# Attention of a two-layer encoder: modulation blocks every third step instead of every second, and the first branch weight block rounded four steps later

## The chip, the cores and the metric

The kernel runs on one core of a Trainium2 chip. The metric is the device time of one execution in microseconds. Three runs of the kernel before took 1734.79 us in the median (1731.39 to 1736.03).

## The reference, cut to what matters

Two groups of 256 tokens each go through two layers with shared weights. Each layer computes six modulation vectors from a small condition vector, then an attention with two branches, then a mixture of experts:

```python
mod = jax.nn.silu(c) @ w_ada + b_ada                     # 1024 x 6144 weights
shift1, scale1, gate1, shift2, scale2, gate2 = split(mod, 6)
h = rms_norm(x, norm_attn) * (1 + scale1) + shift1
qa, ka, va, qb, kb, vb, gates = split(h @ w_in)
ya = gqa_attention(rope(norm(qa)), rope(norm(ka)), va) @ w_branch_a      # branch A: 8 heads of 64
p  = softmax(q1 k1 + bias) - lam * softmax(q2 k2 + bias)                 # branch B: 4 heads, two maps each
yb = (rms_norm(p @ vb, subln_b) * (1 - lam_init)) @ w_branch_b
merged = (sigmoid(g_a) * ya + sigmoid(g_b) * yb) @ w_out
x = x + gate1 * merged
h2 = rms_norm(x, norm_ffn) * (1 + scale2) + shift2
x = x + gate2 * grouped_moe(h2)
```

`shift1` and `scale1` are needed ahead of the attention. `gate1`, `shift2`, `scale2` and `gate2`, two thirds of the product with `w_ada`, are needed only behind it.

## The kernel before, in words

Every engine runs one program in order; engines wait for each other on semaphores. SP issues the weight loads, each of 2 MB, into six slots (`ring`); the order of the blocks is written out in `SLOT`, and a block that reuses a slot is loaded when TensorE has counted the last one there as used.

The product with `w_ada` is cut into 12 blocks of 512 columns. The first four are done ahead of the attention, blocks 4 to 11 in it. A block has three parts. *Rows*: eight accumulating products of 32 output rows each, run as matmuls into one PSUM bank (L750), then ScalarE copies the bank to `tmp` (L1187, function `ada_copy`). *Columns*, one step later: four transposes of `tmp` into another bank (L758). *Sum*, another step later: VectorE adds the four partial rows up into `mod` (L1579, function `ada_sum`), waits for its own result, and gives the bank free (L1581).

The attention is a list of 24 units in 28 steps. Units 0 to 15 belong to branch A (a head pair's half and a token group; one map), units 16 to 23 to branch B (two maps). A step i holds, on TensorE and in this order: the scores of unit i (L887), the turn (transposes) of unit i-2's probabilities (L896), the values product of unit i-3 (L909), for branch B the sum of squares of unit i-4 (`subln`, L914), then the rows of a block if i is in `ADA_STEP`, then the columns of a block if i-1 is. The text calls them scores(i), turn(i), values(i) and subln(i) by the unit.

- ScalarE, step i: copy of turn(i-2) to SBUF (L1277), exponentials of unit i (L1291), the block's copy if i is in `ADA_STEP` (L1187), for branch B the square and the scaled copy of values(i-3) (L1309, L1310), behind which the values bank is given free (L1315), and the square root of subln(i-4) (L1322).
- VectorE, step i: for branch A the maximum of unit i (L1724), for branch B two scaled scores with bias (L1736) and two maxima (L1743); the normalisation of unit i-1 (L1752 to L1766), called norm(i-1), behind which its probabilities are ready (L1769); the copy of values(i-3) for branch A (L1775) and the bank given free (L1777); for branch B the reciprocal of unit i-5 and its product (L1784, L1786); the sum of a block if i-2 is in `ADA_STEP` (L1579); in steps 24 to 27 the low part of a weight group (L1533), whose high part ScalarE makes in the same step (L1147).

A weight is used as a high part, rounded to the matmul's format, and a low part, the rest. For the first group of the branch weights these two stand in the attention's loop as well: ScalarE makes the high part at the head of step `BRANCH_STEP` (L1267), VectorE the low part at the head of the step behind (L1711). The buffer of this high part lies where `tmp` lies, so ScalarE waits there for the columns of the last block (L1271 to L1273).

PSUM has eight banks here. Scores go through banks 0 to 3 in turn, turns and block rows through 4 and 5, values, subln and block columns through 6 and 7. Which bank a use gets follows from the order of the steps alone (`psum_uses`), and TensorE waits in front of each use until the engine that read the bank's last use has given it free.

Behind the attention VectorE finishes the modulation (L1586, L1591) and makes four low parts of branch A's output (L1798); TensorE has two gate products (L719 to L721) to run in the meantime, then the first branch product, which needs those low parts. The products of the merge follow.

Of the kernel before, what the change touches and what calls it, by code (L numbers as in the profile page):

```python
# [70 lines left out]
ADA = MC * P // 512  # L71
ADA_FIRST = 2 * KC // 4
# [106 lines left out]
LAG = {"scores": 0, "turn": 2, "values": 3, "subln": 4}  # L179
ATT_STEPS = N_UNITS + LAG["subln"]  # L180

ADA_STEP = {2 + 2 * n: ADA_FIRST + n for n in range(ADA - ADA_FIRST)}

QKV_ORDER = ["qa0", "qa1", "qa2", "qa3", "ka", "va", "qb0", "turn_va", "rope0", "qb1", "rope1", "qb2", "rope2",
             "qb3", "rope3", "kb0", "rope4", "kb1", "kb2", "kb3", "vb0", "vb1", "vb2", "vb3"]
# [8 lines left out]
def attention_steps():  # L194

    for i in range(ATT_STEPS):
        for stage, back in LAG.items():
            u = i - back
            if 0 <= u < N_UNITS and not (stage == "subln" and UNITS[u][0] == "A"):
                yield i, stage, u  # L200
        if i in ADA_STEP:
            yield i, "ada_rows", ADA_STEP[i]
        if i - 1 in ADA_STEP:
            yield i, "ada_cols", ADA_STEP[i - 1]

# [7 lines left out]


MERGE_AHEAD = 1
BRANCH_STEP = 21


def merge_order():
# [105 lines left out]
def build_trunk(nc, t_in, y_prompt, y_sample):  # L325
# [8 lines left out]
    with ctx:  # L334
# [211 lines left out]
        def wait_full(eng, use, key):  # L546

            b, n = use[key]
            eng.wait_ge(full[b], n + 1)
            return bank[b]  # L550
# [527 lines left out]
        def _(act):  # L1078
# [103 lines left out]
            def ada_copy(i):  # L1182

                ps = wait_full(act, layer_use, ("ada_rows", i))
                if i >= 2:
                    wait_full(act, layer_use, ("ada_cols", i - 2))
                nc.scalar.copy(tmp[:, i % 2, :], ps[:, :]).then_inc(S["ada_rows"], 1)  # L1187
                act.wait_ge(S["ada_rows"], i + 1)
                nc.scalar.sem_inc(free[layer_use[("ada_rows", i)][0]], 1)

            for layer in range(DEPTH):
# [78 lines left out]
                for i in range(ATT_STEPS):  # L1270
                    if i == BRANCH_STEP:  # L1271
                        wait_full(act, use, ("ada_cols", ADA - 1))
# [8 lines left out]
                    if i < N_UNITS:  # L1281
# [14 lines left out]
                        if maps == 1:  # L1296
                            act.wait_ge(S["exp_done"], u + 1)
                            nc.scalar.sem_inc(free[use[("scores", u, 0)][0]], 1)
                    if i in ADA_STEP:
                        ada_copy(ADA_STEP[i])  # L1300
                    u = i - LAG["values"]
# [164 lines left out]
        def _(dve):  # L1466
# [154 lines left out]
            for layer in range(DEPTH):  # L1621
# [83 lines left out]
                def branch_low(n):  # L1705

                    gate, _, j = steps[n]
                    cols = slice(j * P, (j + 1) * P)
                    at = SLOT["br" + gate[1]]
                    dve.wait_ge(S["br_hi_ready"], n + 1)  # L1710
                    v.tensor_tensor(w_lo[at][:, :].rearrange("p (k n) -> p k n", k=4)[:, :, cols],  # L1711
                                    ring[at][:, :].rearrange("p (k n) -> p k n", k=4)[:, :, cols],
                                    br_hi[:, n % 2, :, :].bitcast(F32), ALU.subtract).then_inc(S["br_lo_ready"], 1)

                for i in range(ATT_STEPS + 1):
                    if i == BRANCH_STEP + 1:
                        branch_low(0)
# [454 lines left out]
```

## Time and profile before

| | |
|---|---|
| median of 3 runs | 1734.79 us |
| the profiled execution | 1732.43 us, its span 1730.5 us |
| granted TensorE clock, mean | 0.941 |
| busy: TensorE, VectorE, ScalarE | 86%, 61%, 51% of the span |
| attention of layer 0 | from 179.2 us (first scores) to 306.41 us (first branch product) |
| first branch product of layer 1 | 1136.65 us |

The rows below are of the one profiled execution, the time of which stands beside its span. In a row of the timeline come the start, the duration, the engine, the line with its operation, what it writes and reads, its shape, how many such instructions the row merges, and in brackets the idle time of the engine in front of it with what ended that. "DVEq L1581" is a semaphore step of VectorE's queue at that line. In a row by stretch come the stretch, its length, the busy time and number of instructions of TensorE, its weight loads, VectorE, ScalarE and GpSimd, then the granted clock, the DMA engines' busy share and GB/s. The clock column is the granted clock as a share of 2.4 GHz: 1.00 is that level, 0.50 is 1.2 GHz, and a value between them is a stretch with both.

### The profile page before, as it was taken

To read this page: it belongs to the slowest core of one execution; us is meant where nothing else is said; L and a number is where in the kernel's file an instruction comes from. 1 tells how busy PE (TensorE), PEld (TensorE's weight loads), DVE (VectorE), ACT (ScalarE), POOL (GpSimd) and SP (SyncE) were. 2 spreads that over 40 slices of the span, in tenths; PEclk is the share of its full clock that TensorE was granted. 3 is DMA by queue.
4 is the path that set the end of the run, shared out by engine and by line. 5 is a ranking of instruction groups with operands and counts; after the bars stand their busy time and mean duration, and the time that the engine had idled before them with its cause. 6 is when DMAs were issued, how large, how long until landed. Compare 5 with 4: busy or idle time off the path is not lost.

```text
span 1730.5 us, 19104 instructions
## 1 busy us (share of the span) xinstructions
PE 1482.0 (86%) x6614; PEld 1098.2 (63%) x6614; DVE 1063.4 (61%) x1369; ACT 881.6 (51%) x1186; POOL 127.4 (7%) x145
## 2 busy tenths in 40 slices
PE   3799987999947999999779999699996699999974
PEld 2577545787726777777447754478773577777753
DVE  1464469433466888888275546953355687788845
ACT  3531458323245777777363234842233477777743
POOL 1000000000001122121000000000000111212100
PEclk9899998999978999999889999899997699999996
DMA  9532660113227999999752258011142789999913
GB/s 296 193 111 84 236 202 1 49 49 104 91 106 288 355 370 343 336 347 357 277 157 97 98 180 258 1 49 49 49 146 98 265 314 341 347 358 348 343 61 146
DMA packets 163120, 341.77 MB, mean 198 GB/s; under 512 B 25063, under 2 KB 27265, under 8 KB 162929
## 3 DMA queue, kind: packets, MB, share of 16 engines
q1 hardware_dynamic: 151328, 316.68, 51.9%
q0 software_dynamic: 10992, 23.43, 3.7%
q10 hardware_dynamic: 736, 0.84, 0.2%
q8 instruction: 37, 0.61, 0.1%
q14 instruction: 27, 0.21, 0.0%
HBM read 333.58 MB, written 24.12 MB: 207 GB/s over the span
## 4 chain that ended last, share of the span: by engine, by line
PE 55%; DVE 14%; DMA 12%; issue 9%; ACT 7%; POOLq 2%; SPq 0%; ACTq 0%; DVEq 0%; PEldq 0%; PEld 0%
PE bank L719 10%; PE bank L721 10%; PE bank L720 10%; DMA y_by_choice<-zone,row_now 6%; DMA zone<-rows_by_token,row_now 5%; PE bank L750 2%; PE bank L887 2%; PE bank L1017 2%; PE bank L1019 2%; PE bank L1018 2%; PE bank L909 2%; PE bank L1002 2%; DVE w_lo L2016 1%; PE bank L1004 1%; PE bank L1003 1%
## 5 line engine op out<-in xcount | busy, mean ns | idle before, releaser
L719 PE MATMUL bank<-x_hi,w_lo 128*128 128x512 f32 x608 | 247.4, 407 | 25.3 <-DVE x_lo L1556 16.0
L721 PE MATMUL bank<-x_hi,w_hi 128*128 128x512 f32 x608 | 239.9, 395 | 0.0
L720 PE MATMUL bank<-x_lo,w_hi 128*128 128x512 f32 x608 | 239.8, 394 | 0.0
L2016 DVE TENSOR_TENSOR w_lo<-ring,zone_r 128x2048 fp32r<-128x2048 f32 x92 | 210.4, 2290 | 27.7 <-ACT zone_r L1383 27.7
L1383 ACT CAST x_lo<-ring 128x2048 fp32r<-128x2048 f32 x96 | 184.1, 1919 | 62.5 <-PE bank L1004 26.0
L1383 ACT CAST zone_r<-ring 128x2048 fp32r<-128x2048 f32 x96 | 183.0, 1913 | 24.0 <-PE bank L1019 13.8
L1002 PE MATMUL bank<-w_lo,zone_r 128*128 128x512 f32 x384 | 157.3, 410 | 5.7 <-issue 5.7
L1533 DVE TENSOR_TENSOR w_lo<-ring,w_hi 128x1024 fp32r<-128x1024 f32 x84 | 102.6, 1221 | 87.6 <-ACT w_hi L1147 87.0
L719 PEld LDWEIGHTS bank<-x_hi,w_lo 128*128 128x128 f32 x608 | 115.5, 190 | 62.5 <-issue 25.1
L720 PEld LDWEIGHTS bank<-x_lo,w_hi 128*128 128x128 f32 x608 | 116.1, 191 | 25.5 <-issue 2.4
L721 PEld LDWEIGHTS bank<-x_hi,w_hi 128*128 128x128 f32 x608 | 115.9, 191 | 25.4
L2016 DVE TENSOR_TENSOR w_lo<-ring,x_lo 128x2048 fp32r<-128x2048 f32 x36 | 82.4, 2292 | 43.9 <-ACT x_lo L1383 43.9
L1003 PE MATMUL bank<-x_lo,zone_r 128*128 128x512 f32 x272 | 109.1, 401 | 0.0
L1004 PE MATMUL bank<-x_lo,zone_r 128*128 128x512 f32 x272 | 109.1, 401 | 0.0
L1147 ACT CAST w_hi<-ring 128x1024 fp32r<-128x1024 f32 x84 | 87.5, 1048 | 17.9 <-PE bank L721 6.0
L1004 PE MATMUL bank<-zone_r 128*128 128x512 f32 x240 | 94.3, 393 | 0.0
L1003 PE MATMUL bank<-zone_r 128*128 128x512 f32 x240 | 93.7, 391 | 0.0
L1335 ACT ACTIVATE zone<-bank 128x512 f32<-128x512 f32 x32 | 19.1, 597 | 135.6 <-PE bank L721 135.5
L1002 PEld LDWEIGHTS bank<-w_lo,zone_r 128*128 128x128 f32 x384 | 73.4, 191 | 21.2 <-issue 6.5
L2125 POOL COPY row_now<-row_i 128x1 int32 x60 | 44.7, 745 | 491.1 <-ACT zone L1424 286.9
L2016 DVE TENSOR_TENSOR w_hi<-ring,x_lo 128x2048 fp32r<-128x2048 f32 x32 | 73.5, 2296 | 6.4 <-ACT x_lo L1383 6.1
L2104 POOL DMA_DIRECT2D rows_by_token<-zone x8 | 4.4, 550 | 936.6 <-ACT zone L1370 935.7
(273 smaller groups left out, 2832.1 us busy)
## 6 DMA issues: line engine op xcount, KB each, us to landing
ring<-in_w_gate SPq DMA_DIRECT2D x32, 2048.0 KB
ring<-in_w_up SPq DMA_DIRECT2D x32, 2048.0 KB, 13.9
ring<-in_w_down SPq DMA_DIRECT2D x32, 2048.0 KB, 8.9
ring<-in_w_ada SPq DMA_DIRECT2D x24, 2048.0 KB, 8.8
ring<-in_w_in SPq DMA_DIRECT2D x14, 2048.0 KB, 7.9
ring<-in_w_out SPq DMA_DIRECT2D x4, 2048.0 KB, 7.7
zone<-y_by_choice SPq DMA_DIRECT2D x8, 1024.0 KB, 8.1
ring<-in_w_in SPq DMA_DIRECT2D x16, 256.0 KB, 5.3
```

What stands on the lines that cost most here:

```text
L719: mm(out, lo, x_first, start=start, stop=False)
L720: mm(out, hi, x_second, start=False, stop=False)
L721: return mm(out, hi, x_first, start=False, stop=stop)
L750: ins = mm(ps[32 * j:32 * (j + 1), :], cs[:, k, :], w[:, k, :], start=(k < 4), stop=(k >= KC - 4))
L1002: mm(out, xg_hi[:, par, c, :], wv[:, c, :], start=(c == 0), stop=False)
L1003: mm(out, xg_lo[:, par, c, :], hi[:, k, :], start=False, stop=False)
L1004: ins = mm(out, xg_hi[:, par, c, :], hi[:, k, :], start=False, stop=(c == KC - 1))
L1147: nc.scalar.copy(w_hi[:, n % W_BUFS, :, :], group_view(ring[SLOT[b]], b, c)).then_inc(S["w_hi_ready"], 1)
L1383: nc.scalar.copy(part_hi[buf], ring[EXPERT_SLOTS[par][k]][:, h * 2048:(h + 1) * 2048])\
L1533: v.tensor_tensor(group_view(w_lo[SLOT[b]], b, c), group_view(ring[SLOT[b]], b, c), w_hi[:, n % W_BUFS, :, :].bitcast(F32), ALU.subtract). ...
L2016: v.tensor_tensor(w_low[EXPERT_SLOTS[par][k]][:, cols], ring[EXPERT_SLOTS[par][k]][:, cols], part_hi[buf].bitcast(F32), ALU.subtract)\
L2125: nc.gpsimd.tensor_copy(now, row_i[:, which, bass.ds(tile, 1)]).then_inc(index_now, 1)
```

## The change

Two constants. The blocks' rows, before in steps 2, 4, 6, 8, 10, 12, 14 and 16, stand in steps 2, 5, 8, 11, 14, 17, 20 and 23; columns and sums follow one and two steps later as before. The first branch weight group is rounded at the head of step 25 (ScalarE) and 26 (VectorE) instead of 21 and 22.

```diff
-ADA_STEP = {2 + 2 * n: ADA_FIRST + n for n in range(ADA - ADA_FIRST)}
+ADA_STEP = {2 + 3 * n: ADA_FIRST + n for n in range(ADA - ADA_FIRST)}
...
-BRANCH_STEP = 21
+BRANCH_STEP = 25
```

All engines' loops read these two, and so does the plan of PSUM banks: the order of uses in banks 4 and 5 and in banks 6 and 7 is another one. The loads keep their order in SP's queue, but each waits for a slot that is used up at another step: the gate weights of the first half for blocks 8 and 9, the branch weights for blocks 10 and 11.

## Rows read from the trace of the kernel before

**Rows 1.** Busy time by stretch, layer 0: A steps with blocks, then B steps.

```profile
183.93:238.00 54.07, 53.12 (x306) 26.79 (x305) 27.64 (x89) 26.63 (x77) 0.00 (x0) 1.00 0.76 263
238.00:306.41 68.41, 50.73 (x226) 32.91 (x225) 62.77 (x124) 51.88 (x123) 0.00 (x0) 0.85 0.19 53
```

**Rows 2.** Timeline, TensorE, steps 4 and 5 of layer 0, start of 6.

```profile
191.88 1.92 PE L750 MATMUL bank<-ring,cs 128*32 128x512 f32 x16
193.94 1.12 PE L887 MATMUL bank<-zone 64*128 64x256 f32 x4
...
196.59 0.66 PE L758 MATMUL bank<-const,tmp 128*128 128x128 f32 x4
197.17 1.13 PE L887 MATMUL bank<-zone 64*128 64x256 f32 x4
```

**Rows 3.** Timeline, VectorE, step 5 of layer 0.

```profile
195.10 0.69 DVE L1724 TENSOR_REDUCE nmax<-bank 128x2 f32<-128x512 f32 x1 [2.18 <-PE bank L887]
```

**Rows 4.** Timeline, VectorE, scaled scores of steps 19, 21, 22, layer 0.

```profile
253.99 1.29 DVE L1736 SCALAR_TENSOR_TENSOR zone<-bank,bias 128x512 f32<-128x512 f32 x2 [0.58 <-DVE mod L1579]
...
264.33 1.29 DVE L1736 SCALAR_TENSOR_TENSOR zone<-bank,bias 128x512 f32<-128x512 f32 x2 [1.20 <-PE bank L887]
...
271.79 1.28 DVE L1736 SCALAR_TENSOR_TENSOR zone<-bank,bias 128x512 f32<-128x512 f32 x2
```

**Rows 5.** Timeline, ScalarE, steps 21 and 22, layer 0.

```profile
270.67 0.47 ACT L1310 ACTIVATE zone<-bank,cur 128x256 f32<-128x256 f32 x1
...
273.65 1.28 ACT L1291 ACT_TABLE_LOAD   x1
```

**Rows 6.** Timeline, TensorE, steps 19 to 24, layer 0.

```profile
252.70 0.63 PE L896 MATMUL bank<-const,zone 128*128 128x128 f32 x4 [2.54 <-DVEq L1769]
253.51 1.27 PE L909 MATMUL bank<-zone 128*128 128x256 f32 x4 [0.19 <-DVEq L1581]
...
262.22 2.09 PE L887 MATMUL bank<-zone 64*128 64x256 f32 x8
...
266.72 1.14 PE L887 MATMUL bank<-zone 64*128 64x256 f32 x8
...
271.30 1.97 PE L909 MATMUL bank<-zone 128*128 128x256 f32 x4 [1.69 <-ACTq L1315]
273.13 1.22 PE L914 MATMUL bank<-root,const 128*128 128x256 f32 x2
...
283.29 1.09 PE L896 MATMUL bank<-const,zone 128*128 128x128 f32 x4 [2.88 <-DVEq L1769]
```

**Rows 7.** Timeline, tail of layer 0: a high part, the first branch matmul.

```profile
291.33 1.04 ACT L1147 CAST w_hi<-ring 128x1024 fp32r<-128x1024 f32 x1
...
306.41 0.50 PE L719 MATMUL bank<-zone_r,w_lo 128*128 128x512 f32 x1 [1.63 <-DVE zone_r L1798]
```

**Rows 8.** Busy time by stretch, the merge of layer 0.

```profile
320.00:340.00 20.00, 19.74 (x87) 15.93 (x87) 6.29 (x9) 4.95 (x7) 0.00 (x0) 1.00 0.31 105
```

**Rows 9.** Timeline of layer 1: VectorE, TensorE, ScalarE, steps 19 to 22.

```profile
1084.29 1.29 DVE L1736 SCALAR_TENSOR_TENSOR zone<-bank,bias 128x512 f32<-128x512 f32 x2 [0.23 <-DVE mod L1579]
...
1093.66 1.29 DVE L1736 SCALAR_TENSOR_TENSOR zone<-bank,bias 128x512 f32<-128x512 f32 x2 [0.23 <-DVE zone L1766]
...
1101.13 1.28 DVE L1736 SCALAR_TENSOR_TENSOR zone<-bank,bias 128x512 f32<-128x512 f32 x2
...
1090.81 1.14 PE L887 MATMUL bank<-zone 64*128 64x256 f32 x8
...
1100.98 0.46 ACT L1310 ACTIVATE zone<-bank,cur 128x256 f32<-128x256 f32 x1
```

**Rows 10.** Busy time and granted clock by stretch, layer 0.

```profile
262.00:264.00 2.00, 2.00 (x9) 1.21 (x8) 1.09 (x3) 2.00 (x8) 0.00 (x0) 0.50 0.00 0
...
272.00:274.00 2.00, 2.00 (x5) 0.96 (x4) 2.00 (x4) 1.89 (x4) 0.00 (x0) 0.50 0.00 0
```

**Rows 11.** DMA issues: a branch weight's load, last its us to landing.

```profile
ring<-in_w_branch_b SPq DMA_DIRECT2D x2, 2048.0 KB, 10.2
```

## The prediction, made before the change was run

> **What bounds the kernel now.** I read first the busy times by stretch. In the A steps of layer 0 that hold blocks TensorE is busy 53.12 of 54.07 us, VectorE 27.64 and ScalarE 26.63; from the first B step to the end of attention VectorE is busy 62.77 of 68.41 us and TensorE 50.73, with its granted clock at 0.85 on average [rows 1]. So the attention is two stages with two limits, and the change carries work from the one to the other.
>
> Then the timeline of TensorE in the A stage [rows 2]. A step is scores, turn, values; step 4 takes its block rows at 191.88 and step 5 begins at 193.94, so a block costs 2.06 us there; its columns, in the step behind, cost 197.17 - 196.59 = 0.58 us. There is no wait between these rows: the A stage is TensorE's. Without a block a step is 196.59 - 193.94 = 2.65 us. VectorE idles for 2.18 us behind a block [rows 3] and, at half the stretch's time for both engines [rows 1], it and ScalarE have about 2 us of work in a mean step of 3.97 (half of the pair's 7.94, 2 x 2.65 + 2.06 + 0.58). Both could follow a step of 2.65 us.
>
> Then VectorE in the B stage, where one instruction follows the other nearly without idle time. Two idle times matter: 1.20 us behind TensorE's scores at 264.33, and 0.58 us behind the sum of the block's columns at 253.99 [rows 4]. ScalarE's round is nearly as long, because Exp and Sqrt each need their table: two loads a step, of 1.28 us each [rows 5]. TensorE does wait in the B stage, but in turn for the others: for VectorE's probabilities, and for PSUM banks that ScalarE gives back [rows 6]. After attention the chain runs through VectorE: last normalisations, the modulation's finish, four low parts, and only then the first branch matmul at 306.41, behind 1.63 us of waiting for the last of these [rows 7]. Behind that TensorE is full again (19.74 of 20 us) [rows 8], so a shift of that first branch matmul moves the end by as much. I therefore sum the change at this one instruction, once per layer.
>
> **What is removed: two blocks from the A stage.** Before, rows stand in steps 2, 4 .. 16, columns a step later; after, in 2, 5 .. 23. Seven rows and seven columns become five and five within steps 0 to 15: 2 x (2.06 + 0.58) = -5.3 us per layer [rows 2]. Nothing hides it and nothing takes its place, as the other two engines' 2 us lie under 2.65. The loads of these blocks come no later than needed, since each has more time than before. Row block 16 goes to step 17; scores(17) then come earlier, but VectorE waited for them a few tenths at most. I take 0.
>
> **What is added in B.** Blocks now stand at 17, 20, 23, columns at 18, 21, 24, sums at 19, 22, 25, instead of 16, 17, 18. I follow the chain, numbers in the old trace's times.
>
> Step 19: its sum replaces that of step 18. The sum costs VectorE between 0.34 us (the gap behind it, 0.23, and some tenths for itself, in layer 1) and 0.69 us (0.58, and the same tenths, in layer 0) [rows 4, 9]; I take 0.5. It comes behind norm(18) instead of before it, so TensorE gets the probabilities 0.5 earlier: the chain stands at -5.3 - 0.5 = -5.8.
>
> Step 20: TensorE runs turn(18), values(17), subln(16) and then, before, scores(21), for which VectorE waited 1.20 us in layer 0 [rows 4, 6]. Now block rows stand before scores(21): +2.06 us, or 4.1 at half clock. The clock was 0.50 there until about 264.3 and 1.00 behind [rows 10]; I take 2.06, since the extra block fills the time in which the clock came back. Layer 0 is then at -3.8. In layer 1 scores(21) ran at 1090.81 to 1091.95 and were needed at 1093.66, a slack of 1.7 [rows 9]; there the block costs 0.3: -5.0.
>
> Step 21: the columns. Values, subln and columns take banks 6 and 7 in turn. The order is values(18), subln(17), columns, values(19), subln(18); each waits for the last but one. The columns of step 21 wait until ScalarE has read values(18), at 271.14, and stand ahead of scores(22) in TensorE's queue; these had run at 266.72 already [rows 5, 6]. So scores(22) end 0.1 + 0.58 + 1.1 us behind that read, at 272.9, 1.2 us later than VectorE took them up. The branch block's low part (about 0.65) has left VectorE's queue here. In layer 0 the -3.8 already holds 2.06 of this delay, as the exponentials then follow at once; +0. In layer 1 the read ends at 1101.44 and scores(22) at 1103.2, against 1101.13: +2.1, so -2.9 [rows 9].
>
> Step 22: subln(18) waits for the bank of the columns, which VectorE gives back only with its sum at the end of step 22, behind the 1.75 us reciprocal. Behind subln(18) stand scores(23), the next thing VectorE needs. So VectorE pays the sum, 0.5, and then waits for subln(18) and scores(23): 0.6 + 1.1 + 0.2 = 1.9 at full clock, 1.2 + 2.0 + 0.2 = 3.4 at half. TensorE will have stood idle some 5 us, and after only 1.69 us of it subln(18) took 1.22 us with the clock at 0.50 before [rows 6, 10]; I take 3.4. Layer 0: +0.1. Layer 1: +1.0.
>
> Step 23: rows between subln(19) and turn(22), where TensorE waited 2.88 us in the trace [rows 6]; 2.06 fits. 0, and up to 2 if the clock is halved. ScalarE's copy of the block (0.59) stands behind the exponentials; it has that much to spare while VectorE waits. 0.
>
> Tail: the branch block's low part now stands in step 26: +0.65. Its high part goes from ScalarE's step 21 to step 25, behind a high part that VectorE hardly waits for; 0. The sum of step 25: +0.5. Subln(21) waits for that sum (its bank again), ScalarE's root(21) waits for subln(21), and the next high part (1.04) stands behind the root, and VectorE's low part behind that: 0.6 + 0.42 + 1.04 + three hand-overs of 0.1 = 2.4 us in which VectorE had no wait before [rows 7]. Together +3.5.
>
> Sum: layer 0 +3.6, layer 1 +4.5, in all **+8.1 us**.
>
> DMA: the branch weights' loads go behind blocks 10 and 11, from steps 14 and 16 to steps 20 and 23, about 262 and 283 [rows 11]. The second takes 10.2 us; they are wanted at about 291 and later than 310. Nothing else stands in SP's queue until the merge frees a slot: 0. If the first came late, its cover of 20 us would have to be gone.
>
> All this is against the profiled execution, 1732.43 us, which lies 2.4 under the median 1734.79 of the three. A difference under 0.3% (5.2 us) is about what a measurement of this kernel can't tell from none. 1732.4 + 8.1 = 1740.5.
>
> **Rivals.** (1) *B has room, faster.* TensorE ran ahead of VectorE by up to a step (scores(22) at 266.72, used at 271.79 [rows 4, 6]). If that lead covers the bank waits, what is left is layer 0: -3.8 + 0.5 + 0.5 = -2.8, layer 1: -5.0 + 1.0 = -4.0: 1725.6. It decides from where the two bank waits together cost under 2 us a layer. Against it: values(16) already waited for a sum at 253.51, and values(19) 1.69 us for ScalarE [rows 6]; such waits are real and the new ones stand before scores. Chance 0.1.
>
> (2) *The clock is kept up, no difference.* Blocks put into TensorE's gaps may spare the slow stretch 254 to 264.3 of layer 0, in which the chain ran through TensorE's turn(18), values(17), subln(16) and scores(21): about 3.2 us at full clock (a step's 2.65 and 0.6 for subln), and some 2.4 more there (scores(21) took 2.09 us, scores(22) 1.14) [rows 6, 10]: -2.4; and subln(18) with scores(23) may run at full clock, -1.5 per layer. 8.1 - 5.4 = +2.7: 1735.1. Chance 0.2. The Trainium skill says in "TensorE: Matmul & The Clock Gate", section "Why this matters for your kernels", that throughput drops are avoided by leaving no long idle gaps between bursts of matmuls; by that rule the spread blocks help. The trace agrees as far as it goes: all of the A stage stands at 1.00, and the clock fell in B behind a wait of 2.54 us. But the same rule counts the new 5 us wait against the change.
>
> (3) *Slow clock through most of B, much slower.* Two more long waits of TensorE per layer, each followed by its half clock: rows(20) 2 more, columns and scores(22) 1.7 more, partly in VectorE's shadow; some 3 us a layer: 1746. Chance 0.15.
>
> (4) That the change doesn't do what it says: the steps are constants read by all engines' loops alike, so I leave nothing for it.
>
> **How the numbers follow.** My forecast has 0.55. With the small values everywhere (sum 0.34, full clock) it gives about +4.5, with the large ones +11: 1737 to 1743.5. Rivals (1), (2), (3) have 0.1, 0.2, 0.15. The range leaves out (1) and the far end of (3): 1731 to 1747. Slower by over 0.3%: 0.5 of my 0.55, all of (3), 0.03 of (2): 0.68. Within: 0.05 and 0.17 of (2), 0.22. Faster: 0.1.
>
> **What would show it.** In the changed trace: block rows three steps apart, 2.65 us steps between, the first B scores 5.3 us earlier. TensorE's columns in step 21 waiting for ScalarE's read of values; subln(18) waiting some 5 us for VectorE's sum; VectorE idle 2 to 3.5 us before the two scaled scores of step 23, and about 2.4 us before the second low part in the tail; the first branch matmul 3 to 5 us later than at 306.41. It is wrong if VectorE shows none of these idle times, or if that matmul comes earlier.

## The result, and the profile after

Six runs of the changed kernel took 1742.51 us in the median (1741.91 to 1746.15), six of the kernel before 1733.93 us. The ratio is 1.0051, with a 95% interval of 1.0034 to 1.0069: slower, by about 8.6 us. The forecast was 1740.5 us in a range of 1731 to 1747, 8.1 us slower.

The page of the changed kernel, whose profiled execution took a span of 1740.8 us, has the same number of instructions, and TensorE's busy time (1482.0 us before) is nearly the same:

```profile
span 1740.8 us, 19104 instructions
...
PE 1485.9 (85%) x6614; PEld 1099.8 (63%) x6614; DVE 1063.3 (61%) x1369; ACT 880.9 (51%) x1186; POOL 129.4 (7%) x145
```

The two stretches of the attention of layer 0 (stretch, length, busy time of TensorE, its weight loads, VectorE, ScalarE, GpSimd, then granted clock, DMA share and GB/s), which answer to [rows 1] (the first begins at the same time, which here is 1.4 us ahead of the first block's rows):

```profile
183.93:235.13 51.20, 50.15 (x269) 26.14 (x270) 28.01 (x89) 25.84 (x77) 0.00 (x0) 0.97 0.59 211
235.00:313.37 78.37, 54.85 (x267) 34.52 (x265) 63.14 (x126) 53.29 (x125) 0.00 (x0) 0.85 0.32 95
```

VectorE is busy for 63.14 us of the second stretch, as before. But the stretch is 78.37 us long where the one before had 68.41. The work is nearly the same, and VectorE idles 9.6 us more.

VectorE's timeline shows where. These are its scaled scores of steps 16, 20, 21, 22 and 23 in layer 0; [rows 4] holds those of steps 21 and 22 before:

```profile
235.13 1.29 DVE L1736 SCALAR_TENSOR_TENSOR zone<-bank,bias 128x512 f32<-128x512 f32 x2 [1.13 <-PE bank L887]
...
255.18 1.29 DVE L1736 SCALAR_TENSOR_TENSOR zone<-bank,bias 128x512 f32<-128x512 f32 x2 [0.23 <-DVE mod L1579]
...
261.54 1.29 DVE L1736 SCALAR_TENSOR_TENSOR zone<-bank,bias 128x512 f32<-128x512 f32 x2 [1.90 <-PE bank L887]
...
271.66 1.29 DVE L1736 SCALAR_TENSOR_TENSOR zone<-bank,bias 128x512 f32<-128x512 f32 x2 [3.31 <-PE bank L887]
...
282.07 1.29 DVE L1736 SCALAR_TENSOR_TENSOR zone<-bank,bias 128x512 f32<-128x512 f32 x2 [3.37 <-PE bank L887]
```

The last three each wait for TensorE's scores, 1.90, 3.31 and 3.37 us. What stood ahead of the scores in TensorE's queue is seen in its own timeline, from scores(21) on, which answers to [rows 6]:

```profile
260.38 1.14 PE L887 MATMUL bank<-zone 64*128 64x256 f32 x8
...
268.43 1.11 PE L758 MATMUL bank<-const,tmp 128*128 128x128 f32 x4 [3.99 <-ACTq L1315]
269.48 2.09 PE L887 MATMUL bank<-zone 64*128 64x256 f32 x8
...
278.81 1.22 PE L914 MATMUL bank<-root,const 128*128 128x256 f32 x2 [5.33 <-DVEq L1581]
279.96 2.09 PE L887 MATMUL bank<-zone 64*128 64x256 f32 x8
```

At 268.43 the columns (L758) come after 3.99 us of waiting for ScalarE's step behind its read of values(18) (L1315), and scores(22) follow. At 278.81 comes subln(18), after 5.33 us of waiting for VectorE's step behind the sum (L1581), and then scores(23). Before, scores(22) had no wait ahead of them [rows 6], and scores(23) ran at 274.28, so that VectorE took them up without a wait:

```profile
274.28 1.40 PE L887 MATMUL bank<-zone 64*128 64x256 f32 x8
...
278.63 1.29 DVE L1736 SCALAR_TENSOR_TENSOR zone<-bank,bias 128x512 f32<-128x512 f32 x2
```

In the changed kernel scores(21) run at the high level of the clock, and both pairs behind the bank waits at the low one (a row for each):

```profile
260.00:262.00 2.00, 1.85 (x17) 1.22 (x13) 0.46 (x1) 1.41 (x4) 0.00 (x0) 1.00 0.17 29
...
270.00:272.00 2.00, 2.00 (x11) 1.20 (x8) 0.34 (x1) 0.20 (x1) 0.00 (x0) 0.50 0.84 170
...
280.00:282.00 2.00, 2.00 (x10) 1.19 (x9) 0.00 (x0) 0.47 (x1) 0.00 (x0) 0.50 0.00 0
```

In the tail, subln(21) at 297.31 waits for the sum again; ScalarE's root at 298.05 waits for it, the high part stands behind the root, and VectorE's low part starts only after 2.29 us of waiting for the high part. The first branch matmul of layer 0 comes at 313.37 (ScalarE, VectorE, TensorE; it answers to [rows 7]):

```profile
298.05 0.47 ACT L1322 ACTIVATE root<-bank,eps 128x256 f32<-128x256 f32 x1 [1.55 <-PE bank L914]
298.42 1.03 ACT L1147 CAST w_hi<-ring 128x1024 fp32r<-128x1024 f32 x1
...
299.48 1.23 DVE L1533 TENSOR_TENSOR w_lo<-ring,w_hi 128x1024 fp32r<-128x1024 f32 x1 [2.29 <-ACT w_hi L1147]
...
297.31 0.70 PE L914 MATMUL bank<-root,const 128*128 128x256 f32 x2 [1.60 <-DVEq L1581]
...
313.37 0.50 PE L719 MATMUL bank<-zone_r,w_lo 128*128 128x512 f32 x1 [1.48 <-DVE zone_r L1798]
```

Layer 1 has the same idle times ahead of steps 22 and 23, the first of them larger; its first branch matmul was at 1136.65 before:

```profile
1091.48 1.29 DVE L1736 SCALAR_TENSOR_TENSOR zone<-bank,bias 128x512 f32<-128x512 f32 x2 [0.25 <-PE bank L887]
...
1102.80 1.29 DVE L1736 SCALAR_TENSOR_TENSOR zone<-bank,bias 128x512 f32<-128x512 f32 x2 [4.50 <-PE bank L887]
...
1113.22 1.29 DVE L1736 SCALAR_TENSOR_TENSOR zone<-bank,bias 128x512 f32<-128x512 f32 x2 [3.37 <-PE bank L887]
...
1144.70 0.51 PE L719 MATMUL bank<-zone_r,w_lo 128*128 128x512 f32 x1 [0.82 <-DVE zone_r L1798]
```

A table by step needs an origin that both kernels share. I take the start of scores(3), right behind the first block's rows: 185.99 and 1016.64 us before, 188.27 and 1019.84 us after. From there to VectorE's scaled scores and to the first branch matmul it is, in us:

| | before, layer 0 / 1 | after, layer 0 / 1 | difference | forecast |
|---|---|---|---|---|
| step 16 | 52.15 / 52.15 | 46.86 / 46.85 | -5.3 / -5.3 | -5.3 / -5.3 |
| step 21 | 78.34 / 77.02 | 73.27 / 71.64 | -5.1 / -5.4 | -3.8 / -5.0 |
| step 22 | 85.80 / 84.49 | 83.39 / 82.96 | -2.4 / -1.5 | -3.8 / -2.9 |
| step 23 | 92.64 / 91.34 | 93.80 / 93.38 | +1.2 / +2.0 | +0.1 / +1.0 |
| first branch matmul | 120.42 / 120.01 | 125.10 / 124.86 | +4.7 / +4.9 | +3.6 / +4.5 |

The two layers' sum is 9.5 us. The origin and step 16 of layer 0, before:

```profile
185.99 1.12 PE L887 MATMUL bank<-zone 64*128 64x256 f32 x4
...
238.14 1.29 DVE L1736 SCALAR_TENSOR_TENSOR zone<-bank,bias 128x512 f32<-128x512 f32 x2 [1.13 <-PE bank L887]
```

### The profile page after: what moved, and what is told of

It is laid out like the page before. It is cut to its first block, busy times and chain, and to the rows that moved or that the text cites. A ratio compares the mean times of both kernels' runs of the same rounds, so it can differ in the third digit from the quotient of the medians.

```text
span 1740.8 us, 19104 instructions
## 1 busy us (share of the span) xinstructions
PE 1485.9 (85%) x6614; PEld 1099.8 (63%) x6614; DVE 1063.3 (61%) x1369; ACT 880.9 (51%) x1186; POOL 129.4 (7%) x145
## 4 chain that ended last, share of the span: by engine, by line
PE 54%; DVE 14%; DMA 12%; issue 9%; ACT 7%; POOLq 2%; ACTq 0%; DVEq 0%; SPq 0%
PE bank L719 10%; PE bank L721 10%; PE bank L720 10%; DMA y_by_choice<-zone,row_now 6%; DMA zone<-rows_by_token,row_now 5%; PE bank L887 2%; PE bank L750 2%; PE bank L1017 2%; PE bank L1019 2%; PE bank L1018 2%; DVE w_lo L2016 2%; PE bank L909 2%; PE bank L1002 1%; POOLq L2126 1%; PE bank L1003 1%
```

## The experiments

My theory: the A steps do get 5.3 us shorter, and beside branch B a block costs through waits for PSUM banks that stand ahead of the scores, not through its own time on TensorE. The main rival: block work beside B costs as such, by TensorE's time and clock. All ratios below are against runs of the kernel before on the same chip, with 95% intervals.

**The rounding alone, and the last block at step 17.** The first run moves only the branch group's rounding:

```diff
-BRANCH_STEP = 21
+BRANCH_STEP = 25
```

> The kernel before with only the branch group's rounding moved, from steps 21 and 22 to 25 and 26. Main theory (VectorE's queue is full from step 16 to the first branch product, so its 0.65 us low part costs the same in either place): no difference, within 1 us of the kernel before; scores of step 22 some 0.6 us earlier, the first branch product of layer 0 still some 127.2 us behind the first scores. Rival (the rounding in the tail is what makes the change slower): 3 us or more slower.

Ratio 0.9997 (0.9977 to 1.0018): no difference. VectorE's scaled scores of steps 21, 22 and 23 in this run:

```profile
264.90 1.29 DVE L1736 SCALAR_TENSOR_TENSOR zone<-bank,bias 128x512 f32<-128x512 f32 x2 [1.21 <-PE bank L887]
...
271.75 1.29 DVE L1736 SCALAR_TENSOR_TENSOR zone<-bank,bias 128x512 f32<-128x512 f32 x2
...
278.59 1.29 DVE L1736 SCALAR_TENSOR_TENSOR zone<-bank,bias 128x512 f32<-128x512 f32 x2
```

Step 22 follows step 21 by 6.85 us instead of 7.46: the low part has left that place. The first branch matmul is 120.41 and 120.05 us behind scores(3), as before (120.42, 120.01), so the tail has it back. As expected.

```diff
+ADA_STEP = {s: ADA_FIRST + n for n, s in enumerate((2, 4, 6, 8, 10, 12, 14, 17))}
```

(`BRANCH_STEP = 25` in this and the next two.)

> As branch25, and the last block's rows in step 17 instead of 16 (columns 18, sum 19); the other blocks as before. Main theory (a block costs only where TensorE's queue or a bank wait stands ahead of scores that VectorE needs, and at 17 to 19 TensorE is ahead): no difference, within 1.5 us. Rival (every block beside branch B's units costs its TensorE time of 2.6 us per layer): it stood beside them before too, so no difference either; this run fixes the base for the next two.

Ratio 1.0002 (0.9984 to 1.0020); by the trace the first branch matmuls come 0.6 and 0.1 us earlier than before. As expected.

**One block at step 20, or at step 23.**

```diff
+ADA_STEP = {s: ADA_FIRST + n for n, s in enumerate((2, 4, 6, 8, 10, 12, 14, 20))}
```

> As branch25, and the last block's rows in step 20 (columns 21, sum 22), so one block with the two bank waits of steps 21 and 22 and nothing taken out of the A steps. Main theory (bank waits through VectorE's and ScalarE's queues): 4.7 to 8 us slower per layer, 9 to 16 us in all; VectorE idle ahead of the scaled scores of steps 21 (2 us), 22 (1 to 4 us) and 23 (1.9 to 3.4 us). Rival (a block beside B costs its TensorE time only): at most 2.6 us per layer, 5 us in all, and no idle time ahead of step 23.

Ratio 1.0070 (1.0043 to 1.0097), 12 us slower; by the trace 7.0 and 7.5 us per layer from scores(3) to the first branch matmul (127.39 and 127.55). One block, with nothing taken from the A steps, brings all three idle times ahead of scores, and both bank waits (VectorE, then TensorE's columns and subln(18)):

```profile
262.70 1.29 DVE L1736 SCALAR_TENSOR_TENSOR zone<-bank,bias 128x512 f32<-128x512 f32 x2 [2.15 <-PE bank L887]
...
272.82 1.29 DVE L1736 SCALAR_TENSOR_TENSOR zone<-bank,bias 128x512 f32<-128x512 f32 x2 [3.31 <-PE bank L887]
...
283.23 1.29 DVE L1736 SCALAR_TENSOR_TENSOR zone<-bank,bias 128x512 f32<-128x512 f32 x2 [3.37 <-PE bank L887]
...
269.60 1.11 PE L758 MATMUL bank<-const,tmp 128*128 128x128 f32 x4 [3.99 <-ACTq L1315]
...
279.97 1.22 PE L914 MATMUL bank<-root,const 128*128 128x256 f32 x2 [5.70 <-DVEq L1581]
```

The rival allowed 5 us in all and no idle time ahead of step 23.

```diff
+ADA_STEP = {s: ADA_FIRST + n for n, s in enumerate((2, 4, 6, 8, 10, 12, 14, 23))}
```

> As branch25, and the last block's rows in step 23 (columns 24, sum 25). Main theory (the bank wait of subln(21) on the sum, and the high and low parts queued behind it): 3.0 to 3.6 us slower per layer, 6 to 7 us in all; VectorE idle 2.3 us ahead of its second low part. Rival (TensorE has room there, the block fits in its gap): within 1.5 us of the kernel before, the sum's half a microsecond per layer.

Ratio 1.0036 (1.0016 to 1.0055), 6 us slower; 3.1 and 2.6 us per layer. VectorE's step 23 has no wait, its second low part waits 2.81 us for ScalarE's high part:

```profile
275.78 1.29 DVE L1736 SCALAR_TENSOR_TENSOR zone<-bank,bias 128x512 f32<-128x512 f32 x2
...
295.16 1.23 DVE L1533 TENSOR_TENSOR w_lo<-ring,w_hi 128x1024 fp32r<-128x1024 f32 x1 [2.81 <-ACT w_hi L1147]
```

The four runs nearly close the sum. Per layer the block at 20 costs 7.0 and 7.5 us more than at 16, the one at 23 costs 3.1 and 2.6 more, and two blocks fewer in the A steps give 5.3: +4.8 and +4.8. The changed kernel has +4.7 and +4.9. The close match is in part chance. In last20 and last23 the block is moved, so the small price of a block at 16 (its sum, 0.34 to 0.69 us in the kernel before) is missing in both figures; and ahead of step 21 last20 waits 2.15 and 2.25 us, the changed kernel 1.90 and 0.25.

**Other banks, or an earlier sum.** The next runs take the changed kernel and remove what makes TensorE wait. First the columns go to banks 4 and 5:

```diff
-        elif stage in ("turn", "ada_rows"):
+        elif stage in ("turn", "ada_rows", "ada_cols"):
             yield (stage, u), (4, 5)
```

> The changed kernel with the columns of the attention's blocks in PSUM banks 4 and 5 (with turns and rows) instead of 6 and 7 (with values and subln). Main theory (the cost is the bank waits): VectorE's idle times of 3.3 us ahead of step 22, 3.4 us ahead of step 23 and 2.3 us ahead of the second low part vanish; in the A steps turns now wait at times for the sum, so of the 5.3 us gained there 3.4 are left; about 1 us per layer faster than the kernel before, 2 us in all, some 10 us faster than the changed kernel. Rival (block work beside branch B costs as such, through TensorE's time and clock): as the changed kernel, some 8 us slower than before, the idle times still there.

Ratio 0.9960 (0.9940 to 0.9979): 6.9 us faster than the kernel before, where 2 were expected. By the trace it is 2.4 us per layer. The same block work stands at the same steps, and the idle times ahead of steps 22 and 23 and of the second low part are gone; columns and subln(18) no longer wait for a bank (VectorE's steps 21 to 23, then TensorE):

```profile
262.41 1.29 DVE L1736 SCALAR_TENSOR_TENSOR zone<-bank,bias 128x512 f32<-128x512 f32 x2 [2.18 <-PE bank L887]
...
269.26 1.29 DVE L1736 SCALAR_TENSOR_TENSOR zone<-bank,bias 128x512 f32<-128x512 f32 x2
...
276.52 1.29 DVE L1736 SCALAR_TENSOR_TENSOR zone<-bank,bias 128x512 f32<-128x512 f32 x2 [0.23 <-DVE mod L1579]
...
265.16 0.60 PE L758 MATMUL bank<-const,tmp 128*128 128x128 f32 x4
...
271.13 1.22 PE L914 MATMUL bank<-root,const 128*128 128x256 f32 x2 [0.66 <-ACT root L1322]
```

That decides against the rival. The wait of 2.18 us ahead of step 21, scores behind the block's rows, is what remains. The amount was missed in the A steps: I expected turns to wait for sums there and to leave 3.4 of the 5.3 us, but step 16 is 47.19 us behind scores(3), 5.0 us earlier than before.

```diff
                 for i in range(ATT_STEPS + 1):
+                    if i - 2 in ADA_STEP:
+                        ada_sum(own, ADA_STEP[i - 2])
                     if i == BRANCH_STEP + 1:
...
-                    if i - 2 in ADA_STEP:
-                        ada_sum(own, ADA_STEP[i - 2])
```

> The changed kernel with the banks as they are and each block's sum at the head of VectorE's step instead of its end, so that the bank comes free before the normalisation and the 1.75 us reciprocal. Main theory: subln(18) and subln(21) find their bank free; the idle time ahead of step 23 and ahead of the second low part goes, the one ahead of step 22 (columns behind ScalarE's read of values(18)) stays in part; 0.5 to 2.2 us per layer faster than the kernel before, 1 to 4 us in all. Rival: as the changed kernel, 8 us slower than before.

Ratio 0.9978 (0.9962 to 0.9994), 3.8 us faster than before; by the trace 1.3 and 0.8 us per layer. The wait ahead of step 23 has gone (277.55 has none), and the one ahead of step 22 stands, now split around the sum: 1.31 us until the columns are there, 1.74 until the scores are (the edit moves the later lines by two):

```profile
260.65 1.29 DVE L1738 SCALAR_TENSOR_TENSOR zone<-bank,bias 128x512 f32<-128x512 f32 x2 [2.24 <-PE bank L887]
...
268.78 0.19 DVE L1579 TENSOR_REDUCE mod<-bank 128x8 f32<-128x32 f32 x1 [1.31 <-PE bank L758]
270.71 1.29 DVE L1738 SCALAR_TENSOR_TENSOR zone<-bank,bias 128x512 f32<-128x512 f32 x2 [1.74 <-PE bank L887]
...
277.55 1.29 DVE L1738 SCALAR_TENSOR_TENSOR zone<-bank,bias 128x512 f32<-128x512 f32 x2
```

So the two bank waits are two things. The one on the sum goes with either edit; the one on ScalarE's read of values(18) only with the other banks. Both edits together:

> The two edits of cols45 and sumfirst together on the changed kernel. Main theory: the 5.3 us of the A steps are kept whole and none of the three idle times is left; paid are the two more sums and scores(21) behind the rows: 3.7 us per layer faster than the kernel before, 7.4 us in all. Rival: not faster than the kernel before.

Ratio 0.9964 (0.9949 to 0.9979); by the trace 3.8 and 4.1 us per layer, as expected. By the ratios it can't be told from the run with other banks alone.

**Is it the edits, or the steps?** The same two edits with the old steps 2, 4 .. 16:

> The kernel before, its steps as they were, with the two edits of the run both (columns in banks 4 and 5, sum at the head of VectorE's step). Main theory (the gain is the TensorE time taken out of the A steps; banks and the sum's place only remove the price beside B, and here there is none): within 1 us of the kernel before. Rival (the two edits are faster by themselves, whatever the steps): 3 us or more faster.

Ratio 1.0001 (0.9988 to 1.0014), and by the trace 0.0 us in both layers: nothing. The gain comes from work taken out of the A steps; banks and the sum's place only take away its price.

**How much fits beside branch B?** With both edits, more blocks are moved:

```diff
+ADA_STEP = {s: ADA_FIRST + n for n, s in enumerate((2, 5, 8, 11, 17, 19, 21, 23))}   # four_b, four_b_old_banks
+ADA_STEP = {s: ADA_FIRST + n for n, s in enumerate((2, 6, 10, 17, 19, 21, 22, 23))}   # five_b
+ADA_STEP = {s: ADA_FIRST + n for n, s in enumerate((16, 17, 18, 19, 20, 21, 22, 23))}   # all_b
```

> As both, with blocks' rows in steps 2, 5, 8, 11, 17, 19, 21, 23: four beside branch B's units, four in the A steps. Main theory (TensorE has room beside B once no bank wait stands ahead of scores): the A steps lose a third block, 2.6 us more per layer, of which the fourth sum takes some tenths: 6 to 6.7 us per layer faster than the kernel before, 12 to 13.4 us in all. Rival (B's room is used up at three): as the run with both edits or slower.

Ratio 0.9935 (0.9911 to 0.9958), 11.3 us faster; 6.7 and 5.6 us per layer by the trace, at or a little under what was expected. The same steps with the columns back in banks 6 and 7:

> As four_b but with the columns back in banks 6 and 7, so with only the sum moved. Main theory: one bank wait is left, the columns behind ScalarE's read of values; VectorE idle 0.5 us to 2 us ahead of one of its scaled scores; 2 to 3 us per layer slower than four_b, 4.4 us per layer (9 us in all) or less faster than the kernel before. Rival (with the sum at the head of the step the banks no longer matter): as four_b, 11 us faster than before.

Ratio 0.9971 (0.9954 to 0.9987), 5 us faster than before. With one edit less, VectorE waits again for columns and scores, 2.28 and 1.81 us around a sum:

```profile
257.25 0.19 DVE L1579 TENSOR_REDUCE mod<-bank 128x8 f32<-128x32 f32 x1 [2.28 <-PE bank L758]
259.25 1.29 DVE L1738 SCALAR_TENSOR_TENSOR zone<-bank,bias 128x512 f32<-128x512 f32 x2 [1.81 <-PE bank L887]
```

Its first branch matmuls are 119.00 and 117.73 us behind scores(3), 5.3 and 3.3 us later than with the other banks, more than the 2 to 3 I gave. I had expected an idle time ahead of one of the scaled scores; there is a second, 1.73 us ahead of step 23.

> As four_b, with blocks' rows in steps 2, 6, 10, 17, 19, 21, 22, 23: five beside branch B's units, three in the A steps. Main theory: one more block out of the A steps, 2.6 us per layer, little of it given back: 8 to 8.8 us per layer faster than the kernel before, 16 to 17.6 us in all. Rival (B's room ends at four; rows in three steps in a row make TensorE or ScalarE late): no faster than four_b, 11 us faster than before.

Ratio 0.9916 (0.9902 to 0.9929), 14.6 us faster; 8.4 and 7.9 us per layer by the trace, a little under the 16 to 17.6 in all.

> As five_b, with all eight blocks' rows in steps 16 to 23, one a step, none in the A steps. Main theory (the A steps are TensorE's, B has room): 7 x 2.64 = 18.5 us leave the A steps of a layer, a third of it comes back through ScalarE's copies (0.59 each), the sums and scores behind rows: 11 to 13 us per layer faster than the kernel before, 22 to 26 in all. Rival 1 (B's room is used up at five, ScalarE becomes the limit): about as five_b, 15 us. Rival 2 (the loads of the blocks, 2 MB each, can't keep up with a block per step): TensorE waits at rows for a load, as five_b or slower.

Ratio 0.9851 (0.9826 to 0.9876): 1708.37 us in the median against 1733.62, 26 us faster. This is the version that beats both kernels. No row of TensorE waits for a load in its attention, which decides against the second rival. From the first scores to the first branch matmul it takes 115.35 and 115.74 us, from 178.69 and 997.81 us on (127.18 and 128.15 before). From 220 to 290 us, nearly its B stage, TensorE is busy 59.85 of 70 us with the clock at 1.00 (columns as above):

```profile
220.00:290.00 70.00, 59.85 (x367) 33.73 (x366) 61.39 (x128) 54.09 (x129) 0.00 (x0) 1.00 0.73 241
```

```profile
294.04 0.50 PE L719 MATMUL bank<-zone_r,w_lo 128*128 128x512 f32 x1 [1.69 <-DVE zone_r L1798]
...
1113.55 0.50 PE L719 MATMUL bank<-zone_r,w_lo 128*128 128x512 f32 x1 [1.58 <-DVE zone_r L1798]
```

## Why the prediction was right, step by step

*The A steps: -5.3.* Measured -5.29 and -5.30 us in the two layers. TensorE was the limit, and the other two engines followed a step of 2.65 us.

*Step 19, its sum in place of step 18's: -0.5.* VectorE's scaled scores of step 20 come 5.8 us earlier than before in layer 0, as forecast, and 5.4 in layer 1. My sum for layer 1 has a slip at this place: -5.8 and a block at 0.3 make -5.5, not -5.0. Its terms as they stand give +4.0 for layer 1 and 7.6 us in all, not 8.1.

*Step 20, the rows ahead of scores(21): taken at 2.06 in layer 0 and 0.3 in layer 1.* Too dear in layer 0: the chain at step 21 stands at -5.1 where -3.8 was forecast. VectorE's wait went from 1.20 to 1.90 us only, since the clock was up at 260.38 (scores(21) took 1.14 us, before 2.09). That is the mechanism of the second rival, in this one place, worth 1.3 us. In layer 1 the rows cost nothing: scores(21) were there 0.25 us behind VectorE's last instruction.

*Step 21, the columns: taken at 0 in layer 0 and 2.1 in layer 1.* This is the term that was mis-sized: it measured 2.7 and 3.9 us. The wait on the bank was there, for the reason given, but I priced the columns at 0.58 and scores(22) at 1.1 us, both at full clock. They took 1.11 and 2.09 us at 0.50, behind an idle time of 3.99 us (3.63 in layer 1), which is 1.5 us more. The argument that layer 0 held this delay already fell too, since step 20 had not brought the delay.

*Step 22, subln(18) behind the sum: 0.5 for the sum and 3.4 of waiting.* VectorE waited 3.37 us in both layers, and the step cost 3.6, where 3.9 were forecast. Here the low clock was assumed, and it came.

*Step 23: 0.* The rows took 1.92 us and turn(22) waited 0.60 us behind them: they fit.

*Tail: +3.5.* Measured +3.5 and +2.8. The low part's wait was 2.29 us against 2.4.

*Branch rounding and DMA: 0.* The run branch25 shows the first. No row of TensorE waits for a load in the changed kernel's attention.

The terms off in size cancel in part: the sum per layer is +4.7 and +4.9 against +3.6 and +4.5. Every wait that was forecast came, where it was forecast; but that the total lies within about 1 us is in part luck, as the columns were 2.7 and 1.8 us too cheap, and the rows of step 20 and the tail too dear.

*The rivals.* That B has room was wrong for this kernel, by its own test: the two bank waits cost over 6 us a layer. But its premise is right once the waits are gone, as all_b shows. That the clock would be kept up came true for scores(21) alone; the bank waits themselves brought it down again. A slow clock through most of B did not come: it is 0.85 in the B stage of either layer, where it was 0.85 and 0.90 before.

## What to carry to other kernels

When work is moved into an engine's idle time, ask first what it will wait for and what stands behind it in that engine's queue, not how long it takes: here 2.6 us of work cost 7 us at one step and nothing three steps earlier. A PSUM bank is part of the schedule; where banks go round by the order of use, a new use changes the partner of every later wait. Remove those couplings (another bank, the reader moved to the head of its step), and then move as much as fits.

## What the runs showed of the hardware that I had not expected

The start of the attention has two speeds in one kernel. Behind the first three scores TensorE waits 2.18 us in either layer. In the changed kernel's layer 0 the turn behind that wait takes 1.09 us, and scores(3) start 8.12 us behind scores(0):

```profile
184.28 1.09 PE L896 MATMUL bank<-const,zone 128*128 128x128 f32 x4 [2.18 <-DVEq L1769]
...
188.27 1.12 PE L887 MATMUL bank<-zone 64*128 64x256 f32 x4
```

In its layer 1, with the same instructions and the same wait, the turn takes 0.63 us, and it is 6.76 us:

```profile
1017.22 0.63 PE L896 MATMUL bank<-const,zone 128*128 128x128 f32 x4 [2.18 <-DVEq L1769]
...
1019.84 1.12 PE L887 MATMUL bank<-zone 64*128 64x256 f32 x4
```

In the kernel before it was the other way round: 6.76 us in layer 0, 8.14 in layer 1. From the turn to scores(3) the granted clock is 0.64 on average in the first case and 1.00 in the second. A layer thus gains or loses about 1.4 us by whether the clock falls there. The text of the program doesn't decide it: the kernel before, branch25, last17, last20 and last23 are the same up to this place in layer 0, and it is 6.76, 6.75, 8.38, 6.77 and 6.76 us there. A difference between two profiles should be read from behind such a place. In all_b, where no block's rows stand behind this turn, the low clock lasts longer, in both layers: scores(3) take 2.07 us.

The other surprise is the clock beside branch B. Before it was 0.85 in that stage of layer 0 and 0.90 in layer 1, and with a block in each of steps 16 to 23 it is 1.00 in both. The blocks stand in the gaps behind which it fell. How much of the 26 us comes from that was not tried apart. The Trainium skill says in "TensorE: Matmul & The Clock Gate", section "Why this matters for your kernels", that throughput drops are avoided by leaving no long idle gaps between bursts of matmuls; the changed kernel agrees with it (3.99 and 5.33 us of waiting, then 0.50). The length of a single wait doesn't settle it here, though: TensorE waits 2.70 us in the B stage of all_b's layer 1, ahead of 1098.06, and the clock stays at 1.00, while in the kernel before it fell behind a wait of 2.54 us [rows 6], and at the start of an attention it fell behind 2.18 us.
